# Tiled weights in HBM, 2 MB transfers and a reordered expert block in a hybrid encoder with 32 experts

## The reference

```python
h = rmsnorm(x, norm1_g)
qa, ka, va, qb, kb, vb, ga, gb = split(h @ w_in + b_in)        # w_in 1024 x 4352
oa = neighborhood_attention(qa, ka, va, rpb)                   # 8 heads, 4 x 64 grid
ob = sliding_window_gqa(rope(qb), rope(kb), vb, sinks)         # 8 heads, 2 of keys
x = x + (sigmoid(ga) * (oa @ w_up_a) + sigmoid(gb) * (ob @ w_up_b)) @ w_out
h2 = rmsnorm(x, norm2_g)
top_v, top_i = top_k(h2 @ w_router + b_router, 4); gates = softmax(top_v)
for each token and each e of its four experts, weighted by its gate:
    gu = h2 @ w1[e] + b1[e]                                    # w1[e] 1024 x 2048
    gate, up = min(gu[:1024], 7), clip(gu[1024:], -7, 7)
    x += gate_e * (((up + 1) * gate * sigmoid(1.702 * gate)) @ w2[e] + b2[e])   # w2[e] 1024 x 1024
return rmsnorm(x, final_g)
```

## Time and profile before

| | |
|---|---|
| three runs | 1179.8, 1182.62, 1183.21 us; median 1182.62 |
| profiled execution, span | 1179.72 us (no other time of that execution is given; the lowest run is 0.1 us above it) |
| PE busy, share of the span | 1085.5 us, 92% |
| DVE, ACT, POOL busy | 250.2, 139.9, 16.3 us |
| moved by DMA | 436.41 MB (of 10^6 bytes), mean 370 GB/s |
| w1 matmuls (L731), w2 matmuls (L753) | 456.0 us, 226.8 us busy |
| projections (L489) | 104.7 us busy |

### The profile page before, as it was taken

How to read it: one execution, slowest core, us unless ns; L and a number is a source line. 1 busy time by engine, 2 the same in 40 slices (tenths; PEclk the granted TensorE clock), 3 DMA queues, 4 the chain that set the end, 5 groups by cost and what they waited for, 6 DMA issues and landing times.

```text
span 1179.7 us, 13808 instructions
## 1 busy us (share of the span) xinstructions
PE 1085.5 (92%) x5169; PEld 480.0 (41%) x5169; DVE 250.2 (21%) x531; ACT 139.9 (12%) x267; POOL 16.3 (1%) x21
## 2 busy tenths in 40 slices
PE   7999999999999999998888888988888999999996
PEld 6887778633333333332222322332323333333332
DVE  2253432321111121111111111111111112111112
ACT  0021320210000000000000000000001111111111
POOL 0200000200000000000000000000000000000000
PEclk9999999999999999999999999999999999999999
DMA  9983385589999999999999999999999999999994
GB/s 276 301 299 108 97 344 191 183 356 364 418 418 418 418 418 417 418 417 418 418 418 417 417 418 418 417 417 418 418 418 419 418 419 419 419 419 418 419 417 159
DMA packets 105509, 436.41 MB, mean 370 GB/s; under 512 B 14562, under 2 KB 36500, under 8 KB 72628
## 3 DMA queue, kind: packets, MB, share of 16 engines
q1 hardware_dynamic: 105492, 436.18, 92.9%
HBM read 435.10 MB, written 1.05 MB: 370 GB/s over the span
## 4 chain that ended last, share of the span: by engine, by line
PE 57%; DMA 17%; SPq 14%; DVE 8%; issue 3%; ACT 1%; POOL 0%; DVEq 0%; POOLq 0%; ACTq 0%
PE bank L731 21%; DMA ring<-in_w 17%; PE bank L753 13%; PE bank L489 9%; SPq L386 7%; SPq L371 7%; PE bank L699 3%; PE bank L574 2%; PE bank L610 2%; DVE work L1072 1%; DVE work L1074 1%; DVE work L1077 1%; PE bank L657 1%; DVE work L1070 1%; PE bank L485 1%
## 5 line engine op out<-in xcount | busy, mean ns | idle before, releaser
L731 PE MATMUL bank<-ring,work 128*64 128x512 f32 x2048 | 456.0, 596 | 19.5 <-DMA ring<-in_w 18.8
L731 PEld LDWEIGHTS bank<-ring,work 128*64 128x64 f32 x2048 | 140.3, 137 | 328.3 <-issue 265.6
L753 PE MATMUL bank<-ring,work 128*64 128x512 f32 x1024 | 226.8, 595 | 4.1
L1069 DVE TENSOR_SCALAR work<-bank 128x512 f32<-128x512 f32 x32 | 22.1, 692 | 505.1 <-PE bank L731 505.1
L753 PEld LDWEIGHTS bank<-ring,work 128*64 128x64 f32 x1024 | 70.7, 137 | 139.6 <-issue 127.9
L489 PE MATMUL bank<-hT,ring 128*128 128x256 f32 x464 | 104.7, 386 | 0.8 <-DVE hT L820 0.8
L1192 ACT ACTIVATE work<-work 128x512 f32<-128x512 f32 x32 | 20.2, 630 | 705.7 <-DVE work L1069 705.7
L489 PEld LDWEIGHTS bank<-hT,ring 128*128 128x128 f32 x464 | 88.6, 193 | 16.6 <-issue 1.9
L657 PE MATMUL bank<-cst,work 128*128 128x128 f32 x324 | 42.6, 278 | 36.4 <-DVE work L1074 36.2
L699 PE MATMUL bank<-work 64*128 64x512 f32 x256 | 63.6, 615 | 11.7 <-DVE work L1080 11.7
L1080 DVE COPY work<-bank 128x512 f32<-128x512 f32 x32 | 22.1, 692 | 230.1 <-PE bank L753 230.1
(11 more groups left out here) (176 smaller groups left out, 450.4 us busy)
## 6 DMA issues: line engine op xcount, KB each, us to landing
ring<-in_w SPq DMA_DIRECT2D x374, 1024.0 KB, 20.5
ring<-in_w_in SPq DMA_DIRECT2D x17, 1024.0 KB, 11.8
held<-in_w SPq DMA_DIRECT2D x10, 1024.0 KB, 7.7
ring<-in_w_out SPq DMA_DIRECT2D x4, 1024.0 KB, 5.2
ring<-in_w_up_a SPq DMA_DIRECT2D x2, 1024.0 KB, 10.3
ring<-in_w_up_b SPq DMA_DIRECT2D x2, 1024.0 KB, 8.1
tables<-in_na_rpb SPq DMA_DIRECT2D x16, 96.0 KB, 4.7
held<-in_x SPq DMA_DIRECT2D x2, 512.0 KB, 3.8
```

What stands on the lines that cost most here:

```text
L731: last = pe.matmul(bank[CAP * a:CAP * (a + 1), bk, :], kT, ring[:, s, q * 512:(q + 1) * 512], start=False, stop=k == W1_CH - 1)
L753: last = pe.matmul(bank[CAP * a:CAP * (a + 1), BH, :], fT, ring[:, s, f % 2 * D + a * 512:f % 2 * D + (a + 1) * 512], start=f == 0, stop=f ...
```

## The change

1. **Layout.** A host-side function `tiles_of` reorders the bytes of w_in, w_up_a, w_up_b, w_out, w1 and w2 once, before the launch, into the order in which the kernel reads them. A chunk before the experts is then one run of 8 KB per partition; an expert's 12 MB are six pairs of chunks, with one run of 16 KB per partition each.
2. **Pairs.** The ring is seen as 6 pairs of 2 MB. An expert is 6 transfers (4 of w1, 2 of w2), each with a semaphore of its own, and a pair is released when both its halves are used. `HELD` is now 5 pairs, so the last five experts load 5 of 6 pairs; the bytes that are held stay 10 MB. The copy by ScalarE is 128 x 4096 instead of 128 x 2048.
3. **Order.** TensorE's scatter of the block before comes behind w1 instead of ahead of it, and the four turns of the gathered rows stand between the fourth and fifth f-step of w2.

```diff
-W1_CH, W2_CH = D // P, FF // (2 * P)
-HELD = 10
-HELD_EARLY = 6
+PAIR_F = 2 * SLOT_F
+PAIRS = SLOTS // 2
+W1_CH, W2_CH = D // (2 * P), FF // (4 * P)
+HELD = 5
+HELD_EARLY = 3
...
+        def pair_of(c):
+            return (c + 1) % PAIRS
+
+        def used_before(blk, c):
+            if isinstance(blk, int) and blk == 0:
+                return PRE - SLOTS + 1 + 2 * pair_of(c) + 1 if c < PAIRS - 1 else PRE
+            return (blk - 1) * BLK + PRE + c + 1
...
             def load_expert(e, blk, has_held=False):
-                one = bass.ds(e, 1)
                 for c in range(BLK - 1 if has_held else BLK):
-                    sp.wait_ge(chunk_used, blk * BLK + PRE + c - SLOTS + 1)
-                    s = expert_slot(c)[0]
-                    if c < W1_CH:
-                        src = w1[0, one, c * P:(c + 1) * P, :].rearrange("e p n -> p (e n)")
-                        sp.dma_start(ring[:, s, :], src).then_inc(landed[s], 16)
-                    else:
-                        chunk_of_w2(e, c, ring[:, s, :]).then_inc(landed[s], 16)
+                    sp.wait_ge(chunk_used, used_before(blk, c))
+                    sp.dma_start(pairs[:, pair_of(c), :], pair_source(e, c)).then_inc(pair_landed[c], 16)
...
             def expert_block(b, first=False):
                 if not first:
                     add_b1(b)
-                    pe.wait_ge(down_ready, b)
-                    pe.wait_ge(scatT_ready, b + 1)
-                    scatter()
                 pe.wait_ge(xgT_ready, b + 1)
-                for k in range(W1_CH):
-                    s, count = expert_slot(k)
-                    pe.wait_ge(landed[s], b * 16 + count)
+                for k in range(D // P):
+                    if k % 2 == 0:
+                        pe.wait_ge(pair_landed[k // 2], b * 16 + 16)
...
-                    last.then_inc(chunk_used, 1)
+                    if k % 2:
+                        last.then_inc(chunk_used, 1)
...
+                if not first:
+                    pe.wait_ge(down_ready, b)
+                    scatter()
                 pe.wait_ge(pick_ready, b + 2)
                 gather()
                 pe.wait_ge(hid_ready, b + 1)
                 turn(BH, lambda j: hid[:, j * P:(j + 1) * P], 4, hidT_done)
                 pe.wait_ge(pick_g_ready, b + 1)
                 turn(BU, lambda m: pick_g[:, m, :], MT, scatT_done)
-                pe.wait_ge(xg_ready, b + 2)
-                turn_gathered()
...
+                    if f == TURN_F:
+                        pe.wait_ge(xg_ready, b + 2)
+                        turn_gathered()
...
+def tiles_of(inputs):
+    def rows_and_columns(w, n, width):
+        return w.reshape(-1, P, n, width).transpose(2, 1, 0, 3).reshape(n, P, SLOT_F)
+
+    def row_groups(w, n):
+        return w.reshape(E, n, -1, P, w.shape[-1]).transpose(0, 1, 3, 2, 4).reshape(E, n, P, PAIR_F)
```

More of the change, by code:

```diff
@@ L137, in build_block @@
         h2 = hT[:].rearrange("p k t -> p (k t)").rearrange("p (m d) -> p m d", m=MT)
-        held = sb("held", [P, HELD, SLOT_F])
+        held = sb("held", [P, HELD, PAIR_F])
+        pairs = ring[:].rearrange("p (s two) n -> p s (two n)", two=2)
         arena = held[:].rearrange("p s n -> p (s n)")
-        left, right = [0], [HELD * SLOT_F]
+        left, right = [0], [HELD * PAIR_F]
         def attn_buf(n):
@@ L153, in build_block @@
         g2_b = late_buf(D)
-        UNTIL_NORM2 = 2
+        UNTIL_NORM2 = 1
         wr = late_buf(KD * E).rearrange("p (k e) -> p k e", e=E)
@@ L190, in build_block @@
         vec_rows = attn_buf(P)
-        assert left[0] <= right[0] and HELD_EARLY * SLOT_F <= right[0]
+        assert left[0] <= right[0] and HELD_EARLY * PAIR_F <= right[0]
         n_vec = D_IN // P + 2 * KD
@@ L242, in build_block @@
         landed = [sem(f"chunk_landed{n}") for n in range(SLOTS)]
+        pair_landed = [sem(f"pair_landed{n}") for n in range(PAIRS)]
         chunk_used = sem("chunk_used")
@@ L280, in landings @@
             return 16 * (chunk // SLOTS + 1)
-        def expert_slot(c):
-            return slot_of(PRE + c), landings(PRE + c)
+        def pair_of(c):
[4 more added lines that the diff above has]
+            return (blk - 1) * BLK + PRE + c + 1
         BLK = W1_CH + W2_CH
-        assert BLK == SLOTS and N_IN * CW == D_IN
+        assert PRE == 2 * SLOTS + 1
+        assert BLK == PAIRS and N_IN * CW == D_IN
         UNITS = HEADS
@@ L326, in chunk_source @@
                 if n < N_IN:
-                    return w_in[0, :, n * CW:(n + 1) * CW].rearrange("(k p) n -> p k n", p=P)
+                    return w_in[n]
                 n -= N_IN
                 if n < N_UP:
-                    w = (w_up_a, w_up_b)[n % 2]
-                    return w[0, :, n // 2 * 512:(n // 2 + 1) * 512].rearrange("(k p) n -> p k n", p=P)
+                    return (w_up_a, w_up_b)[n % 2][n // 2]
                 n -= N_UP
-                return w_out[0, :, n * CW:(n + 1) * CW].rearrange("(k p) n -> p k n", p=P)
+                return w_out[n]
             for n in range(PRE):
@@ L337, in _ @@
                     sp.wait_ge(chunk_used, n - SLOTS + 1)
-                src = chunk_source(n)
-                dst = ring[:, slot_of(n), :].rearrange("p (k n) -> p k n", n=src.shape[2])
-                sp.dma_start(dst, src).then_inc(landed[slot_of(n)], 16)
+                sp.dma_start(ring[:, slot_of(n), :], chunk_source(n)).then_inc(landed[slot_of(n)], 16)
                 if n == 2:
@@ L365, in _, with pair_source @@
                         sp.dma_start(b1_raw[part * E:(part + 1) * E, :], b1[0]).then_inc(b1_landed, 16)
[L367 to L371, removed]
+            def pair_source(e, c):
+                w, at = (w1, c) if c < W1_CH else (w2, c - W1_CH)
+                return w[bass.ds(e, 1), at].rearrange("e p n -> p (e n)")
             def load_held(first, last):
                 for n in range(first, last):
-                    chunk_of_w2(E - HELD + n, BLK - 1, held[:, n, :]).then_inc(held_landed, 16)
+                    sp.dma_start(held[:, n, :], pair_source(E - HELD + n, BLK - 1)).then_inc(held_landed, 16)
             def load_expert(e, blk, has_held=False):
-                one = bass.ds(e, 1)
                 for c in range(BLK - 1 if has_held else BLK):
-                    sp.wait_ge(chunk_used, blk * BLK + PRE + c - SLOTS + 1)
-                    s = expert_slot(c)[0]
-                    if c < W1_CH:
-                        src = w1[0, one, c * P:(c + 1) * P, :].rearrange("e p n -> p (e n)")
-                        sp.dma_start(ring[:, s, :], src).then_inc(landed[s], 16)
-                    else:
-                        chunk_of_w2(e, c, ring[:, s, :]).then_inc(landed[s], 16)
+                    sp.wait_ge(chunk_used, used_before(blk, c))
+                    sp.dma_start(pairs[:, pair_of(c), :], pair_source(e, c)).then_inc(pair_landed[c], 16)
             sp.wait_ge(o_ready, UNITS)
@@ L709, in _ @@
             LIST_K = [0, 2, 4]
+            TURN_F = 4
             def add_b1(b):
@@ L721, in expert_block @@
                     add_b1(b)
-                    pe.wait_ge(down_ready, b)
-                    pe.wait_ge(scatT_ready, b + 1)
-                    scatter()
                 pe.wait_ge(xgT_ready, b + 1)
-                for k in range(W1_CH):
-                    s, count = expert_slot(k)
-                    pe.wait_ge(landed[s], b * 16 + count)
+                for k in range(D // P):
+                    if k % 2 == 0:
+                        pe.wait_ge(pair_landed[k // 2], b * 16 + 16)
+                    at = k % 2 * SLOT_F
                     kT = xgT[:, (k % 4) * P + k // 4 * CAP:(k % 4) * P + (k // 4 + 1) * CAP]
                     for q, (bk, a) in enumerate(parts):
-                        last = pe.matmul(bank[CAP * a:CAP * (a + 1), bk, :], kT, ring[:, s, q * 512:(q + 1) * 512],
-                                         start=False, stop=k == W1_CH - 1)
-                    last.then_inc(chunk_used, 1)
+                        last = pe.matmul(bank[CAP * a:CAP * (a + 1), bk, :], kT,
+                                         pairs[:, pair_of(k // 2), at + q * 512:at + (q + 1) * 512],
+                                         start=False, stop=k == D // P - 1)
+                    if k % 2:
+                        last.then_inc(chunk_used, 1)
                     if first and k in LIST_K:
                         list_blocks(LIST_K.index(k))
+                if not first:
+                    pe.wait_ge(down_ready, b)
+                    scatter()
                 pe.wait_ge(pick_ready, b + 2)
@@ L742, in expert_block @@
                 turn(BU, lambda m: pick_g[:, m, :], MT, scatT_done)
-                pe.wait_ge(xg_ready, b + 2)
-                turn_gathered()
                 pe.wait_ge(hidT_ready, b + 1)
[L747 to L750, removed]
+                for f in range(FF // P):
+                    c = W1_CH + f // 4
+                    if f % 4 == 0:
```

(27 more changed lines are left out.)

## The result

The changed kernel takes 1174.1 us (median of 4 runs, 1173.49 to 1174.93) where the kernel before took 1182.0 (4 runs): a ratio of 0.9941, 95% interval 0.9927 to 0.9954, so 0.6% faster. The forecast was 1171 us, 1160 to 1188. The profiled execution has a span of 1173.0 us and took 1174.93, so 1.9 us lie around the span. Six further runs of the changed kernel have a median of 1173.08 against 1180.03 on the same chip, ratio 0.994 [0.9923, 0.9958].

A forecast was written before the change was run, and what follows sets the result against it. DMA was taken to bound 21 to 22 experts, PE the last ten. Longer runs -23 to -24 us, order -3 to -4, held pairs and release +13 to +16 gave a 1168.0 us span, forecast 1171, range 1160 to 1188.

The forecast's parts named there:

- Longer runs: Experts' weight stream: 16 KB runs cut a 2 MB pair from 5.02 to 4.87 us, -23 to -24 us in all.
- rival A: Experts' weight stream: DMA splits 16 KB runs into two 8 KB packets, 4.96 us a pair, 1185 us; chance 17%.
- the start of the stream: Effective start of the experts' DMA stream: 251.6 us before, 253.6 after, as a pair's release needs both slots, 2.0 us later.
- A rule against it: Skill's DMA bandwidth figures against the run-length term: by one, 2 MB takes about 4.93 us, end some 10 us later.
- rival C: Experts' weight stream: half as many transfers also halve each one's end cost, 4.78 us a pair, 1157 us; chance 14%.
- rival B: Weight stream doesn't speed up: 5.02 us a pair, 1195 us; from 4.97 held pairs make it slower; chance 17%.
- Held pairs and release: Relief for only the last five experts, and slots released in pairs: cost of 13 to 16 us together.
- Order: TensorE's expert block: scatter behind w1, four turns inside w2, 28.04 to 27.15 us where PE bounds; -3 to -4 us.
- the new wait of 0.56: Start of w2 on TensorE: a new wait for VectorE's copy L1077, some 0.6 us.
- hidden turns: TensorE's block: lower bound of 26.6 us if the turns ahead of w2 are hidden as well.
- Rival D: TensorE's new order gains nothing, turn inside w2 breaks the matmul stream: some +3 us, 1174; within the forecast's 52%.
- Start, ScalarE: Early weights' 8 KB runs: 0 us, as PE doesn't wait; ScalarE's held copy grows to some 3.8 us, costing nothing.

The follow-up runs named there:

- natural rows: Changed kernel with w1 and w2 in natural layout (runs of 8 and 4 KB), still 2 MB transfers: 1192.67 us, ratio 1.0092 to the kernel before.
- half transfers: Changed kernel, still tiled, each pair loaded by two 1 MB transfers with runs of 8 KB: 1186.41 us, ratio 1.0039 to the kernel before.
- spread halves: Changed kernel with the same 10 MB held as ten 1 MB halves over the last ten experts: 1160.69 us, ratio 0.9825 to the kernel before.

## Why the prediction was right

*Longer runs.* The mechanism held and the runs weren't split (rival A): of the 41124 packets 27,888 have 8 KB or more, while split runs alone would make 49,152. The term was mis-sized by little: 4.87 us per pair forecast, 29.38 / 6 = 4.90 measured. I had taken 0.09 us as the price of 8 runs, from a step of 2.48 us that was rounded; at 9.2 ns each they cost 0.074, so the data take 2 x 2.41 and not 2 x 2.39. Over 160 pairs the 0.027 makes 4.3 us, and w1 of block 27 ended at 1041.3, not 1036.4. That is most of the miss in the span (1173.0 against 1168.0); the rest is in the start of the stream, which comes out at 254.3 by my arithmetic, not 253.6. From there to the end I had 131.6 us, and it was 131.7. The estimate of 4.93 us per 2 MB in "A rule against it" was nearly right too: 4.90 lies between it and my 4.87.

*Luck.* I had no term for the clock, and the same kernel's other profile, with the early rise and no fall in block 1, ends w1 of block 27 at 1037.6. The sum missed by 4.9 us in one execution and by 1.2 in the other. And from span to median I added 2.9 us; the median is 1.1 above this span, whose execution was the slowest of its four. So 5.0 us of miss in the span left 3.2 in the median.

*The number of transfers* (rival C) is refuted by the natural rows: 2 MB transfers with old runs have the old rate. *No faster stream* (rival B) is refuted by 429 GB/s, and the half transfers refute its reason: runs from a contiguous tile, cut to 8 KB, cost as much as w1's rows did. But B's second part, that the price of the held pairs decides the sign, is shown: at 29.82 us per expert, 4.97 per pair, the kernel is slower than before by 0.4%.

*Held pairs and release*, forecast at 13 to 16 us. Natural rows against before give 13.1 us at an equal pace of DMA, and with the 1.9 us of the order added back 15. Of this the held part is 11.1 us, measured by the spread halves. The release wasn't tried alone; the first pair of block 0 was issued at 245.89, 2.6 us behind the 243.32 of the kernel before, where I had 2.0.

*Order.* PE's block was forecast at 27.15 us and is 27.14; the new wait of 0.56 was forecast at 0.6. The block's match is partly two misses that cancel: w2 with the turns in it takes 7.8 us, not 7.54, and w1 takes 13.73, not 13.91. The order's worth was forecast at 3 to 4 us. That was a slip in the sum: four blocks at 0.84 less the 1.32 that it adds to the tail make 2.0. Measured are 2.8 on the old kernel, and on the new one 1.3 between medians and 1.9 in the profiles. Inside it are two edits of opposite sign, which I hadn't priced apart: the scatter behind w1 gains (a block at PE's pace falls from 28.03 to 26.41 us with it alone), and the turns inside w2 lose 0.73 of that per block, about 4 us in all. The prediction saw that w2 waits for VectorE's copy anyway, and had hidden turns only as a bound of 26.6; it didn't draw from the wait that turns ahead of w2 are free. Rival D had the sign of the turns right, yet as a loss of the whole gain, and its + 3 us has the same slip.

*Start, ScalarE.* No effect of the early layout, as forecast. ScalarE's copy takes 3.62 us and nobody waits for it.

## What to carry to other kernels

When a stream of weights is the bound, count runs, not transfers: here a contiguous run of 4, 8 or 16 KB cost about 9 ns on its DMA engine beyond its bytes, and halving the number of transfers did nothing. Spread preloaded data over so many stages that DMA and the compute engine are just balanced in each; given in bulk to the last five, the same bytes were worth 11 us less. Before moving work out of a wait, look at what the wait hides: the four turns were free ahead of w2, where PE had to wait for the copy, and cost 0.7 us per block inside it.

## What the runs showed that was not expected

- One program has two groups of times, 1171.2 and 1175.0 us here. Its two profiles differ by 1.8 us in the first projections, by when the granted clock first is at its upper level (11.0 or 15.3 us after the start), and by 1.7 us in w1 of block 1, where the granted clock was at its lower level for part of it in one of them. A difference of 2 to 4 us between kernels needs runs enough to see both groups: four runs were misread by 3 us.
- A run cost about 9 ns going from 4 to 8 KB and 9.2 ns going from 8 to 16 KB; 429 GB/s is the highest rate held over hundreds of us, and longer runs weren't tried.
